# The front of a two-layer block: w_ada in f32 on two column groups instead of split halves, with the early tiles and the ctx rows in a new order

## The reference, cut to what matters

```python
sc, scc = jax.nn.silu(c), jax.nn.silu(c_ctx)
shift, scale, gate = jnp.split(sc @ w_ada[l] + b_ada[l], 3, axis=-1)
shift_c, scale_c, gate_c = jnp.split(scc @ w_ada[l] + b_ada[l], 3, axis=-1)
hc = _rmsnorm(ctx, g_pre[l]) * (1.0 + scale_c) + shift_c
zc = hc @ w_in[l][:, :XBC_W + DT_W]
hx = _rmsnorm(x, g_pre[l]) * (1.0 + scale[:, None]) + shift[:, None]
zx = hx @ w_in[l]
```

## Time and profile before

| | us |
|---|---|
| median of three runs | 2802.37 |
| profiled execution, span of the page | 2803.5 |
| TensorE busy in it | 2755.5 (98%) |
| VectorE busy | 1539.7 (55%) |
| ScalarE busy | 1124.7 (40%) |
| GpSimd busy | 331.9 (12%) |

### The profile page before, as it was taken

One profiled execution on the slowest core, in us unless ns is written; L12 is line 12 of the kernel. 1 busy time (PEld: TensorE's weight loads), 2 busy tenths in 40 slices (PEclk: granted clock), 3 DMA queues, 4 the chain that ended last, 5 costly groups with the idle time before them and its releaser, 6 DMA issues. The chain is left out here.

```text
span 2803.5 us, 33298 instructions
## 1 busy us (share of the span) xinstructions
PE 2755.5 (98%) x13110; PEld 2243.4 (80%) x13110; DVE 1539.7 (55%) x1862; ACT 1124.7 (40%) x1484; POOL 331.9 (12%) x409
## 2 busy tenths in 40 slices
PE   6999999999999999999999999899999999999999
PEld 2688888878888888888888888788888888788787
DVE  6867678674555546666753233544445544533733
ACT  7742222234343333333332332436656553442611
POOL 1011100000334124322311000100000000000000
PEclk8999999999999999999999999999999999999999
DMA  9647767654455554455455333242222223223252
GB/s 398 242 171 271 245 249 276 234 213 145 143 167 175 163 177 149 152 177 188 143 170 209 110 119 105 84 142 84 89 76 83 83 83 109 86 90 98 97 181 91
DMA packets 162122, 439.35 MB, mean 157 GB/s; under 512 B 14768, under 2 KB 59824, under 8 KB 151728
## 3 DMA queue, kind: packets, MB, share of 16 engines
q1 hardware_dynamic: 123360, 307.28, 33.0%
q0 software_dynamic: 15792, 92.99, 9.4%
q10 hardware_dynamic: 22816, 36.97, 3.7%
HBM read 398.11 MB, written 39.06 MB: 156 GB/s over the span
## 5 line engine op out<-in xcount | busy, mean ns | idle before, releaser
L1641 DVE TENSOR_TENSOR WL<-RAW,WH 128x1024 fp32r<-128x1024 f32 (+1 forms) x424 | 516.3, 1226 | 745.0 <-ACT WH L1009 574.7
L414 PE MATMUL PB<-HH,WH 128*128 128x512 f32 x2048 | 816.8, 399 | 5.0 <-DVE WL L1641 3.8
L419 PE MATMUL PB<-HL,WH 128*128 128x512 f32 x2048 | 802.0, 392 | 0.0
L420 PE MATMUL PB<-HH,WL 128*128 128x512 f32 x2048 | 801.9, 392 | 0.0
L1009 ACT ACTIVATE WH<-RAW 128x1024 fp32r<-128x1024 f32 (+1 forms) x424 | 433.6, 1038 | 442.7 <-PE PB L527 257.4
L525 PE MATMUL PB<-WH,HH 128*128 128x512 f32 x1248 | 490.5, 393 | 1.6 <-ACT Kr L1009 0.8
L527 PE MATMUL PB<-WH,HL 128*128 128x512 f32 x1248 | 486.6, 390 | 0.0
L526 PE MATMUL PB<-WL,HH 128*128 128x512 f32 x1248 | 486.4, 390 | 0.0
L414 PEld LDWEIGHTS PB<-HH,WH 128*128 128x128 f32 x2048 | 385.2, 188 | 93.4 <-issue 10.8
L419 PEld LDWEIGHTS PB<-HL,WH 128*128 128x128 f32 x2048 | 386.2, 189 | 65.5 <-issue 3.3
L420 PEld LDWEIGHTS PB<-HH,WL 128*128 128x128 f32 x2048 | 385.6, 188 | 66.0
(11 more groups left out here) (324 smaller groups left out, 2704.3 us busy)
## 6 DMA issues: line engine op xcount, KB each, us to landing
RAW<-in_w_in_t SPq DMA_DIRECT2D x320, 512.0 KB, 3.7
AU<-in_w_ada POOLq DMA_DIRECT2D x64, 1024.0 KB, 5.5
RAW<-in_w_out_t SPq DMA_DIRECT2D x96, 512.0 KB, 3.7
bcb<-R SPq DMA_DIRECT2D x64, 256.0 KB, 6.3
S<-so ACTq DMA_DIRECT2D x24, 384.0 KB, 2.4
ebc<-R SPq DMA_DIRECT2D x32, 256.0 KB, 6.0
SY<-evb ACTq DMA_DIRECT2D x32, 256.0 KB, 2.6
yin<-SY POOLq DMA_DIRECT2D x32, 256.0 KB, 4.0
```

The lines of the kernel that those rows point to most:

```text
L414: h.matmul(banks[j], lh, m.HH[:, t, :], start=st, stop=False)
L419: h.matmul(banks[j], lh, m.HL[:, t, :], start=False, stop=False)
L420: ins = h.matmul(banks[j], ll, m.HH[:, t, :], start=False, stop=en)
L1641: return h.tensor_tensor(o, a, b, op)
```

## The change

w_ada is no longer split. A unit is two f32 matmuls straight from its place: 32 columns of scs (two of them used, the others zero, line 230 and the new zero-fill) over 512, one for each k-tile, into two groups of 32 rows of bank 5; stages of even and odd number use different pairs of groups. The fold adds the two groups with a matmul by a selector, sel. The columns of w_ada are packed anew, so that a stage gives shift and scale of two tiles t, and turn, modulate and early tiles follow stage by stage. Block 12 (no ctx) comes first in each stage, block 0 second. The turns of ctx come two beats behind those of x. Early halves live in two slots of WH and WL. w_ada has 27 places, which come free when TensorE has used a unit. The rows of x are loaded with units 0 to 3, those of ctx behind units 8 and 9, and RAW 0 to 7 ahead of the units that RAW_AT names. The first early tile is in beat 7, and seven beats with tiles alone follow the units.

```diff
-ADA_ORDER = (0, 4, 1, 5, 2, 6, 3, 7)
-PLACE = list(range(16)) + [16, 17, 18, 19, 22, 23] + list(range(6, 14)) + [20, 21] + \
-    [14, 15, 16, 17, 18, 19, 22, 23, 12, 13, 20, 21, 14, 15, 16, 17] + [18, 19, 22, 23, 20, 21] * 2 + [18, 19, 22, 23]
-BLOCKS = (0, 12) + tuple(range(1, 12)) + (13, 14, 15)
+def places():
+    last = [9, 17, 9, 17, 9, 9, 25, 33, 25, 33, 25, 25, 41, 49, 41, 49, 41, 41, 57, 63, 57, 63, 57, 57, 63, 63, 63]
+    used = [-1] * 27
+    out = []
+    for i in range(64):
+        j = min((j for j in range(27) if last[j] >= i), key=lambda j: (used[j], last[j], j))
+        used[j] = i
+        out.append(j)
+    return out
+PLACE = places()
+RAW_AT = (10, 12, 20, 28, 34, 38, 44, 52)
+BLOCKS = (12, 0) + tuple(range(1, 12)) + (13, 14, 15)
 def beat(k):
-    st = None
-    if 8 <= k <= 32 and k % 8 == 0:
-        st = k // 4 - 1
-    elif 6 <= k < 32 and k % 8 == 6:
-        st = (k - 2) // 4 - 1
-    p, r = divmod(k - 9, 8)
-    t = 4 * p + r if k >= 9 and r < 4 and p < 4 else None
-    return st, t, k - 10 if 10 <= k < 10 + 4 * EARLY else None
-BEATS = 10 + 4 * EARLY
+    st = k // 4 - 1 if k % 4 == 0 and 4 <= k <= 32 else None
+    p, r = divmod(k - 5, 4)
+    t = 2 * p + r if k >= 5 and r < 2 and p < 8 else None
+    return st, t, k - 7 if 7 <= k < 7 + 4 * EARLY else None
+def ctx_beat(k):
+    return beat(k - 2)[1] if k >= 2 else None
+BEATS = 7 + 4 * EARLY
 def early_tile(s):
-    u, tt = divmod(s, 4)
-    return u, BLOCKS[u % 2], tt, 4 * (u // 2) + tt
+    st, r = divmod(s, 4)
+    return 2 * st + r // 2, r // 2, 2 * st + r % 2, r % 2
+def early_half(e):
+    st, b = divmod(e, 2)
+    return 2 * (st // 2) + b, slice(st % 2 * 512, st % 2 * 512 + 512)
+def early_slot(e):
+    return (3, 1)[e % 4 // 2], slice(e % 2 * 512, e % 2 * 512 + 512)
...
-    m.scs = at("scs", WA + 56 * KB, [128, 16, 4], F32R)
+    m.scs = at("scs", 132 * KB, [128, 16, 32])
...
+    for nm, off in ("WHa", 108), ("WHc", 116), ("WLa", 124):
+        m.aus.append(at(f"aus{len(m.aus)}{nm}", off * KB, [128, 1024]))
...
     def a_unit(i):
         st, kk = divmod(i, 8)
-        bank = reuse(5) if kk == 0 else PB[5]
         P.wait_ge(*at("scs"))
-        P.wait_ge(*at("a hi", i))
-        P.wait_ge(*at("a lo", i))
+        P.wait_ge(*at("aus", i))
+        if kk == 0 and st >= 2:
+            P.wait_ge(*at("rowb", st - 2))
         for j in range(2):
-            for part in (m.WH[i % 3], m.WL[i % 3]):
-                ins = h.matmul(bank[0:4, :], m.scs[:, 2 * kk + j, :], part[:, j * 512:(j + 1) * 512],
...
+            r = 64 * (st % 2) + 32 * j
+            ins = h.matmul(PB[5][r:r + 32, :], m.scs[:, 2 * kk + j, :], m.aus[PLACE[i]][:, j * 512:(j + 1) * 512],
+                           start=kk == 0, stop=kk == 7)
...
     def fold(st):
...
+        r = slice(64 * (st % 2), 64 * (st % 2) + 64)
         for j in range(4):
-            ins = h.transpose(PB[7][:, 256 + 4 * j:260 + 4 * j], m.rowb[0:4, j * 128:(j + 1) * 128], ident[0:4, 0:4])
+            ins = h.matmul(PB[7][:, 256 + 2 * j:258 + 2 * j], m.rowb[r, j * 128:(j + 1) * 128], m.C("sel")[r, :],
+                           start=True, stop=True)
...
-        if t is not None:
-            turn_ctx(t)
+        if ctx_beat(k) is not None:
+            turn_ctx(ctx_beat(k))
...
-            u, b, tt, t = early_tile(sub)
-            P.wait_ge(*at("g hi", u, tt // 2))
-            P.wait_ge(*at("g lo", u, tt // 2))
-            first_h(t)
+            e, i, t, r = early_tile(sub)
+            P.wait_ge(*at("g hi", e))
+            P.wait_ge(*at("g lo", e))
+            first_h(t, BLOCKS[i] < 12)
...
-    def a_high(i):
-        A.wait_ge(*at("aus", i))
-        if i >= 3:
-            A.wait_ge(*at("a used", i - 3))
-        act(m.WH[i % 3], m.aus[PLACE[i]], ACT.Copy).then_inc(*put(s.hi, "a hi", i))
...
+    for v in range(4):
+        square_x(v)
     for k in range(BEATS):
         t = beat(k)[1]
+        if t is not None:
+            modulate(t)
+        if k == 5:
+            square_x(4)
+            square_x(5)
+        if ctx_beat(k) is not None:
+            high_ctx(ctx_beat(k))
         sub = beat(k + 2)[2]
         if sub is not None and sub % 2 == 0:
-            early_high(sub)
+            early_high(sub // 2)
...
-    def a_low(i):
-        V.wait_ge(*at("aus", i))
-        V.wait_ge(*at("a hi", i))
-        if i >= 3:
-            V.wait_ge(*at("a used", i - 3))
-        TT(m.WL[i % 3], m.aus[PLACE[i]], m.WH[i % 3].bitcast(F32), ALU.subtract).then_inc(*put(s.lo, "a lo", i))
...
         if before:
-            Y.wait_ge(*at("a hi", before[-1]))
-            Y.wait_ge(*at("a lo", before[-1]))
+            Y.wait_ge(*at("a used", before[-1]))
         elif j in (20, 21):
             Y.wait_ge(*at("x squared", 5))
-        load(m.aus[j], I["w_ada_s"][ADA_ORDER[i // 8] * 8 + i % 8], s.aus[j], "aus", i)
+        load(m.aus[j], I["w_ada_s"][i], s.aus[j], "aus", i)
...
         if 0 <= u - 3 < EARLY:
-            Y.wait_ge(*at("g hi", u - 3, 1))
-            Y.wait_ge(*at("g lo", u - 3, 1))
+            e = 4 * ((u - 3) // 2) + 2 + (u - 3) % 2
+            Y.wait_ge(*at("g hi", e))
+            Y.wait_ge(*at("g lo", e))
...
     for i in range(64):
-        if i >= 16 and i % 8 == 0:
-            raw_load(i // 8 - 2)
+        if i in RAW_AT:
+            raw_load(RAW_AT.index(i))
         ada_load(i)
-        if i % 2 and i < 12:
-            load(m.xs[i // 2], m.x_tile(I, i // 2), s.x[i // 2], "x", i // 2)
-    for u in range(6, 68):
+        if i < 4 or i in (8, 9):
+            v = i if i < 4 else i - 4
+            load(m.xs[v], m.x_tile(I, v), s.x[v], "x", v)
+    for u in range(8, 68):
         raw_load(u)
...
-        "w_ada_s": pack(v["w_ada"][0][:, :4096], 2, 512),
+        "w_ada_s": pack(v["w_ada"][0][:, :4096].reshape(2048, 2, 8, 256).transpose(0, 2, 1, 3).reshape(2048, 4096), 2, 512),
```

More of the change, by code:

```diff
@@ L1027, in scalar_program @@
     A.wait_ge(*t)
-    A.then(act(m.scs[:, :, 0:2], m.scv, ACT.Copy), "scs hi")
+    A.wait_ge(*at("scs zero"))
+    A.then(act(m.scs[:, :, 0:2], m.scv, ACT.Copy), "scs")
     def place_read(j):
-        i = max(i for i in range(64) if PLACE[i] == j)
-        A.wait_ge(*at("a hi", i))
-        A.wait_ge(*at("a lo", i))
-    def a_high(i):
-        A.wait_ge(*at("aus", i))
-        if i >= 3:
-            A.wait_ge(*at("a used", i - 3))
-        act(m.WH[i % 3], m.aus[PLACE[i]], ACT.Copy).then_inc(*put(s.hi, "a hi", i))
+        A.wait_ge(*at("a used", max(i for i in range(64) if PLACE[i] == j)))
     def modulate(t):
@@ L1054, in modulate, with early_high @@
         A.wait_ge(*at("hc", t))
[L1055 to L1059, removed]
+        A.then(act(m.CH[:, t, :], m.hf[t % 2][:, 512:768], ACT.Copy), "CH", t)
+    def early_high(e):
+        u, half = early_half(e)
+        w, place = early_slot(e)
         A.wait_ge(*at("raw", u))
-        if u:
-            A.wait_ge(*at("g used", u - 1, tt // 2))
-        act(m.WH[3][:, half], m.RAW[u % 3][:, half], ACT.Copy).then_inc(*put(s.hi, "g hi", u, tt // 2))
@@ L1065, in scalar_program, with square_x @@
-    junk = None
-    a_high(0)
-    a_high(1)
+        if e >= 4:
+            A.wait_ge(*at("g used", e - 4))
+        act(m.WH[w][:, place], m.RAW[u % 3][:, half], ACT.Copy).then_inc(*put(s.hi, "g hi", e))
+    def square_x(v):
+        A.wait_ge(*at("x", v))
+        if v:
+            A.wait_ge(*at("x squared", v - 1))
+        A.then(act(m.junk, m.xs[v], ACT.Square, acc=m.ss[:, v:v + 1]), "x squared", v)
+    for v in range(4):
+        square_x(v)
     for k in range(BEATS):
         t = beat(k)[1]
[L1070 to L1080, removed]
+        if t is not None:
[5 more added lines that the diff above has]
+            high_ctx(ctx_beat(k))
@@ L1662, in make @@
             low(u, m.RAW[u % 3], "raw", u)
[L1665 to L1666 removed]
+    V.then(h.memset(m.scs, 0.0), "scs zero")
     def place_read(j):
[L1670 to L1679 removed]
+        V.wait_ge(*at("a used", max(i for i in range(64) if PLACE[i] == j)))
@@ L1694, in finish @@
         V.wait_ge(*t)
[L1695 to L1700, removed]
+        V.then(STT(m.Amv[:, c, :], modp[:, 1, c, :], 1.0, m.P("g_pre", 2 * st, 2).unsqueeze(2).to_broadcast([128, 2, 2]),
+                   ALU.add, ALU.mult), "Am", st)
@@ L1727, in vector_program @@
-    a_low(0)
-    a_low(1)
-    for k in range(BEATS):
[L1730 to L1745, removed]
+        V.wait_ge(*at("g hi", e))
@@ new lines, in early_low, with scale_x @@
+        if e >= 4:
+            V.wait_ge(*at("g used", e - 4))
+        TT(m.WL[w][:, place], m.RAW[u % 3][:, half], m.WH[w][:, place].bitcast(F32), ALU.subtract) \
+            .then_inc(*put(s.lo, "g lo", e))
+    def scale_x(v):
+        V.wait_ge(*at("rr", v))
+        V.then(TS(m.xs[v], m.xs[v], m.rr[:, v:v + 1], None, ALU.mult), "xs", v)
+    for v in range(4):
+        scale_x(v)
+    for k in range(BEATS):
+        st, t, _ = beat(k)
+        if st is not None:
+            finish(st)
+        if t is not None:
+            h_low(t)
```

(11 more changed lines are left out.)

79 lines of the change are left out of this document (38 added, 41 removed).

## The result

The changed kernel takes 2811.15 us (median of eight runs, 2808.47 to 2813.04), the kernel before 2802.02 beside it: ratio 1.0032, interval 1.0022 to 1.0042. It is 9.1 us slower; the forecast was 2807.5, or 5.2 slower, so the sign was right and the size about half. Which terms made the difference is what follows. The profiled execution took 2811.34 us, with a span of 2809.6.

The account below looks back on a forecast made before the run. TensorE's own work bounds the front from 58.5 us, the DMA up to some 43. First tile 44.5 + work 123.2 + wait 3.7 + clock 2.0 + hand-over 1.0 = 174.4 against 168.4; 6.0 less 0.8 gives 2807.5 us, range 2790 to 2824.

Parts of the forecast that it names:

- First tile: First early tile in the front: needs unit 15 instead of unit 21, starts at 44.5 us, 14 us earlier.
- Moved ahead and behind: Squares and scalings of x, zero-fill and ctx rows in the DMA-full stage: cost nothing if beat 5 finds x scaled.
- the prediction's own sign of being wrong: A first tile later than 47 us would mean that ACT's squares or the ctx rows hold the turns.
- Clock: Lower granted clock behind waits, at the first tile and unit 52: 0 to 1.7 us each, 1.0 each taken.
- Wait at unit 52: SP holds at RAW 7 for early half 10's split; TensorE waits 3.7 us for unit 52, bounds 0 and 5.
- Hand-over: Front's end: short beats of tiles alone, with last CL, zero-fills and unit 8's low half following closely: 1.0 us, 0 to 2.
- Work of TensorE: Behind the first tile: tiles 56.0, turns 4.9, ctx turns 2.1, units 41.3, form changes 12.6, folds 6.3; 123.2 us.
- The 0.8 of the earlier trace: Behind the front: the 0.81 us wait for the next low half should go, as DVE's two convolutions come earlier.
- Changing the form is free: Rival: changes between column groups and full-width work cost nothing, without 36 x 0.35 = 12.6 us; 2795 us, chance 0.20.
- A pass waits its turn in program order: Rival: only a unit's middle two passes overlap, 0.43 us more in each of 36 stretches; 15.5 us, 2823 us, chance 0.12.
- The groups do not run side by side: Rival: groups of 32 columns do not overlap, 48 x 0.86 = 41 us more; 2848 us, chance 0.06.
- No wait at unit 52: Rival: no wait there and no loss of clock, 5.7 us less, 2802 us; counted within the forecast.

Follow-up runs that it names:

- that with two beats' units: Kernel with a beat's two units on different column groups, changed so that from beat 8 odd beats hold four units and even beats none: 2773.59 us, ratio 0.9899.
- the run on one group: Changed kernel with both matmuls of a unit on the same group of 32 columns, the second adding to the first: 2849.53 us, ratio 1.0167.
- the run with all three: Changed kernel with RAW 7 later, ctx turn ahead of both units, ctx rows scaled earlier, RAW 5 and 6 at units 42 and 48: 2798.86 us, ratio 0.9988.

## Why the prediction came out as it did

The 5.2 us were 6.0 of front less 0.8. Measured, the front is 10.4 us longer (178.7 against 168.3) and the median 9.1; that the median came nearer to the forecast than the front is chance, as the rest of the program varies by more than that. In the profiled execution the main loop starts 4.6 us behind my 174.4, by these steps:

- **First tile: +2.8.** "Moved ahead and behind" is the step that failed. I costed the squares and scalings at nothing as long as the turn of beat 5 finds x scaled, and looked only at the rows of x. The ctx rows are scaled in DVE's beat 6, behind the low half of h, and the ctx turn of beat 7 stands ahead of unit 15. It waited 2.87 us. So the prediction's own sign of being wrong came true, a first tile later than 47 us because the ctx rows hold the turns. The bytes were right: with the scalings earlier the first tile starts at 44.13, against 44.5. The 44.5 need unit 15's load to land at some 43.3 us (44.5 less 0.86 and 0.35), 1.3 later than 16.4 MB take at 391 GB/s. No run shows a reason for that addition: in the changed kernel the loads land one after another, 1.27 us apart, unit 14's at 41.85 and unit 15's at 43.12.
- **Clock: +0.3 at the first tile, +0.5 at unit 52.** I took 1.0 each; they were 1.3 (2.86 less 1.58) and 1.5 (5.41 less 3.87). The granted clock of 0.59 from 47 to 51 us lies between the two levels, 0.5 (1.2 GHz) and 1.0 (2.4 GHz). The rows say which: matmuls 0.42 apart at the first tile are at the lower.
- **Wait at unit 52: +0.2.** Right in place, cause and size. SP goes on 3.5 us into the beat (3.7 foretold), unit 52 starts at 8.4 (8.6), TensorE wants it at 4.9 (4.9); the idle time is 3.87 (3.7). RAW 5 just fits, as said.
- **Hand-over: -0.7.** 0.3 us (178.55 + 0.12 to 178.96), where I put 1.0.
- **Work of TensorE: +1.5.** 131.64 us from first tile to main loop, less 5.41, 1.28 and 0.29, is 124.7; my sum was 123.2. A unit was right at 0.86, a stretch at 0.33 to 0.41 against 0.35, a fold was 0.98 (52.55 to 53.53) against 0.9, which makes 0.6 of it. Some 0.8, one fold included, came in the beats with tiles alone: from the 25th tile at 161.89 us to the main loop are 17.07 us, less 0.3 of hand-over 16.8, against 16.0 by my prices; the seams, which I had counted in the kernel before and left out of this sum, may be that.
- **The 0.8 of the earlier trace rows did not go.** The wait for a low half stands in the changed kernel too, so that credit fell.

The rivals. *Changing the form is free* fell three times: 0.26 in the run with the ctx turn first, 0.33 in that with two beats' units, 0.33 to 0.41 in the rows. The Trainium skill, TensorEngine Tiling (Array Packing), Key Properties, says that a change of tiling mode drains TensorE; the traces agree in that each change has a price, 0.26 to 0.43 us. *A pass waits its turn in program order* fell with the run on one group: sharing saves half of the passes. Units 22 and 23 show it as well: their first passes start 0.01 us apart, the second ones 0.45 later, in pairs again. The Trainium skill, TensorE: Matmul & The Clock Gate, Packing small matmuls, has matmuls start and end strictly in program order. Taken matmul by matmul these rows agree: unit 22 begins and ends ahead of unit 23. But a matmul's two passes don't follow each other as the rival had them, for unit 23's first stands ahead of unit 22's second. *The groups do not run side by side* fell with the same run. *No wait at unit 52* was made true by moving one load, and gave 2803.3, near the 2802 that I had put for it; that it came so near is partly chance, as this run keeps the late first tile.

## What to carry to other kernels

When work moves to an earlier place, look for every consumer that moves with it, not only for the first one: here the second, the ctx turn, found its operand late, and the loss was the wait and the lower clock behind it. On a queue with a fixed order, put a load that waits for a buffer as late as its reader allows, for everything behind it waits too. And profile the kernel before more than once when effects of 0.1% are to be read from two traces: compare stretch by stretch, and trust those that repeat.

## What the runs showed of the hardware

Four column groups of 32 take f32 matmuls of 512 columns as well side by side as two do: 8 passes in 0.86 us (0.43 a pass), found only because units of two stages had overlapped in the changed kernel. Going into such a stretch and out of it costs 0.26 to 0.43 us, the same with four units in it as with two, so gathering them pays (12 changes, 3.93 us). And an idle time on TensorE can cost more than itself, but not by a fixed rate: the lower clock behind it took 1.3 us behind 2.87, 1.5 behind 3.87, nothing behind 2.12 in the run with RAW 7 later, and 2.7 behind 3.5 at unit 52 in the run with the ctx turn first (from the 19th early tile to the 21st 15.14 us, 8.95 in the run with all three).
